# Three-pass fp32r products for 28 more weight units of each mixing layer, with their low parts shared between VectorE and GpSimd

## The reference, cut to what matters

```python
h = rms_norm(x, norm_pre[l]) * (1 + scale) + shift
p = h @ w_in[l]                     # fp32, 1024 rows
(..., r_streams, r_z, g_q, g_k, g_v, g_l, g_z, gate_a, gate_b, gate_c) = split(p)
o_mla = mla_branch(...)             # attention
o_rwkv = rwkv7_branch(...)          # r, k, v, decay and a; a chunked recurrence of 64 tokens
o_gla = gla_branch(...)             # gated linear attention from g_q, g_k, g_v
merged = sigmoid(gate_a)*o_mla + sigmoid(gate_b)*o_rwkv + sigmoid(gate_c)*o_gla
x = x + gate * rms_norm(merged @ w_out[l], norm_post[l])
```

## Time and profile before

| | us |
|---|---|
| median of 3 runs (lowest, highest) | 2012.38 (2011.87, 2013.97) |
| the profiled execution's own time | 2014.74 |
| its span, first to last instruction | 2013.0 |
| TensorE busy | 1929.2 (96%) |
| VectorE busy | 1328.2 (66%) |
| ScalarE busy | 713.8 (35%) |
| GpSimd busy | 97.7 (5%) |
| mean granted TensorE clock | 0.987 of full speed |

### The profile page before, as it was taken

The page is one execution under the profiler, slowest core; times in us unless marked ns, Lnnn a source line. Parts: engine busy times, 40 slices in busy tenths (PEclk is TensorE's granted clock), DMA queues, the critical chain, the costliest instruction groups (busy, mean ns, idle before and its releaser), DMA issues.

```text
span 2013.0 us, 41616 instructions
## 1 busy us (share of the span) xinstructions
PE 1929.2 (96%) x18047; PEld 1783.3 (89%) x18047; DVE 1328.2 (66%) x1722; ACT 713.8 (35%) x1023; POOL 97.7 (5%) x137
## 2 busy tenths in 40 slices
PE   8999999999899999999999999997999998999998
PEld 8988999998599999989887879996998887888997
DVE  7896687747657866864675339676764676428765
ACT  5573433435533331240423123243222234204243
POOL 2000000100400000020000000001002000000000
PEclk9999999999999998999999999998999999999999
DMA  8555478853347794645440236454653540135643
GB/s 216 140 144 157 149 236 266 266 147 116 99 148 258 253 258 106 166 117 154 118 116 6 74 102 173 122 161 104 170 160 102 148 128 22 45 99 147 164 121 111
DMA packets 473063, 291.41 MB, mean 145 GB/s; under 512 B 26679, under 2 KB 467484, under 8 KB 472776
## 3 DMA queue, kind: packets, MB, share of 16 engines
q1 hardware_dynamic: 466688, 262.20, 46.7%
q0 software_dynamic: 5312, 25.32, 3.3%
q10 hardware_dynamic: 904, 1.58, 0.3%
HBM read 288.02 MB, written 1.05 MB: 144 GB/s over the span
## 4 chain that ended last, share of the span: by engine, by line
PE 82%; DVE 13%; ACT 3%; issue 2%; POOL 0%; DMA 0%; DVEq 0%; ACTq 0%; POOLq 0%
PE bank L705 38%; PE bank L1422 6%; PE bank L1424 6%; PE bank L1423 6%; PE bank L694 4%; PE bank L664 2%; DVE rounded L730 2%; PE bank L901 2%; PE bank L893 2%; PE bank L1625 1%; PE bank L1612 1%; PE bank L1068 1%; PE bank L787 1%; PE bank L1474 1%; PE bank L1593 1%
## 5 line engine op out<-in xcount | busy, mean ns | idle before, releaser
L705 PE MATMUL bank<-rounded 128*128 128x256 f32 (+1 forms) x4584 | 564.2, 284 | 12.0 <-DVE rounded L730 9.4
L705 PEld LDWEIGHTS bank<-rounded 128*128 128x128 f32 (+1 forms) x4584 | 550.6, 189 | 21.2 <-DVE rounded L730 14.6
L730 DVE TENSOR_TENSOR rounded<-arena,rounded 128x1024 fp32r<-128x1024 f32 (+1 forms) x251 | 303.4, 1214 | 86.6 <-ACT rounded L719 80.5
L1422 PE MATMUL bank<-parts 128*128 128x256 f32 x1024 | 290.5, 284 | 1.0 <-DVE parts L2226 1.0
L1424 PE MATMUL bank<-parts 128*128 128x256 f32 x1024 | 289.8, 283 | 0.0
L1423 PE MATMUL bank<-parts 128*128 128x256 f32 x1024 | 289.8, 283 | 0.0
L705 PE MATMUL bank<-common,arena 128*128 128x256 f32 x1280 | 285.4, 380 | 0.0
L705 PEld LDWEIGHTS bank<-common,arena 128*128 128x128 f32 x1280 | 240.1, 189 | 39.8 <-issue 4.8
L770 ACT ACTIVATE arena<-bank 128x512 f32<-128x512 f32 x114 | 67.6, 597 | 436.1 <-PE bank L705 423.1
L1422 PEld LDWEIGHTS bank<-parts 128*128 128x128 f32 x1024 | 196.5, 192 | 1.5 <-issue 1.3
L1423 PEld LDWEIGHTS bank<-parts 128*128 128x128 f32 x1024 | 196.6, 192 | 0.1
(11 more groups left out here) (391 smaller groups left out, 2497.9 us busy)
## 6 DMA issues: line engine op xcount, KB each, us to landing
arena<-in_w_in SPq DMA_DIRECT2D x190, 512.0 KB, 3.8
whole<-in_ffn_w_gate_up SPq DMA_DIRECT2D x44, 1024.0 KB, 5.2
arena<-in_ada_w POOLq DMA_DIRECT2D x32, 768.0 KB, 6.3
whole<-in_ffn_w_down SPq DMA_DIRECT2D x16, 1408.0 KB, 7.0
arena<-in_rec_w_in SPq DMA_DIRECT2D x36, 512.0 KB, 3.8
arena<-in_att_w_qkv SPq DMA_DIRECT2D x24, 512.0 KB, 3.7
arena<-in_rec_w_out SPq DMA_DIRECT2D x16, 512.0 KB, 3.7
arena<-in_mla_w_o SPq DMA_DIRECT2D x16, 512.0 KB, 3.8
```

Of the source, the lines that this page charges most:

```text
L705: last = pe.matmul(psum[s][0:c, m % 2 * T:m % 2 * T + T], w[a][:, k, cols], x[b][:, k, :], start=(k, a, b) == (0, 0, 0), stop=k == job.kt ...
L730: dve.tensor_tensor(raw_view(job_of[u], u, UNIT_LOW), raw, high_view(job_of[u], u).bitcast(F32), ALU.subtract)\
L1422: pe.matmul(bank, w_hi, x_hi, start=start and k == 0, stop=False)
```

## The change

Five streams of each mixing layer get parts and three passes: r (8 units), v (8), gb0 (4), gq (4) and gk (4), 28 units in a layer and 56 in all. All their high parts are cast by ScalarE. The low parts of r are made by VectorE; those of the other four, 20 units in a layer, by GpSimd (`low_g`, kind `"shared"`), which has a semaphore of its own. r, v and gb0 use three high buffers of their own (`KEY_HIGHS`), since `SW` lies in the usual ones; `AA` and `CC` move to the places of `KKDD` and `V_`. TensorE takes one more unit of v ahead of the head sums of `RK`. `HX` is made anew ahead of gq, where it was made anew ahead of gv. The casts of ro's units 0 and 1 move from the first half of gk to its second, behind the wait for `gate_in`. The diff, cut to its core:

```diff
+        KEY_HIGHS = [rounded(UNIT, at=aligned() + n * UNIT) for n in range(HIGHS)]
...
         place[0] = lent
-        AA, SW, CC = (buf(DK, T) for _ in range(3))
+        SW = buf(DK, T)
+        assert place[0] <= lent + HIGHS * UNIT
+        AA, CC = KKDD, V_
         place[0] = lent
...
+        def wait_parts_pe(u):
+
+            low = unit_low_g if job_of[u].high == "shared" else unit_low
+            pe.wait_ge(low.sem, low_at[u] + 1)
...
                 done = unit_high if job_of[u].high == "vector" else unit_high_s
                 if done is unit_high:
                     high_parts(dve, dve.tensor_copy, u, unit_high)
-                dve.wait_ge(done.sem, done.due(dve))
+                dve.wait_ge(done.sem, high_at[u] + 1)
...
+
+        def low_g(jobs):
+
+            for u in (u for j in jobs for u in range(j.first, j.first + j.units)):
+                gp.wait_ge(unit_high_s.sem, high_at[u] + 1)
+                raw = raw_view(job_of[u], u, UNIT_RAW)
+                gp.tensor_tensor(raw_view(job_of[u], u, UNIT_LOW), raw, high_view(job_of[u], u).bitcast(F32), ALU.subtract)\
+                  .then_inc(unit_low_g.sem, 1)
...
-            def proj(name, n, high=None, at=0):
-                return Stream(n, 2 * n, HX if high else H, columns(w, IN_AT[name] + at * COLS), high=high)
+            def proj(name, n, high=None, at=0, highs=None):
+                return Stream(n, 2 * n, HX if high else H, columns(w, IN_AT[name] + at * COLS), high=high, highs=highs)
...
-                "k": proj("k", 4, "vector"), "r": proj("r", 4), "v": proj("v", 4),
-                "gb0": proj("gb", 2), "gb1": proj("gb", 1, at=2), "gb2": proj("gb", 1, at=3),
+                "k": proj("k", 4, "vector"), "r": proj("r", 4, "scalar", highs=KEY_HIGHS), "v": proj("v", 4, "shared", highs=KEY_HIGHS),
+                "gb0": proj("gb", 2, "shared", highs=KEY_HIGHS), "gb1": proj("gb", 1, at=2), "gb2": proj("gb", 1, at=3),
                 "rz0": proj("rz", 2), "rz1": proj("rz", 1, at=2), "rz2": proj("rz", 1, at=3),
-                "gq": proj("gq", 2), "gk": proj("gk", 2),
+                "gq": proj("gq", 2, "shared"), "gk": proj("gk", 2, "shared"),
...
-        split_left = [list(split_units)]
+        by_gpsimd = [u for u in split_units if job_of[u].high == "shared"]
+        by_vector = [u for u in split_units if job_of[u].high != "shared"]
+        low_at = {u: i for units in (by_gpsimd, by_vector) for i, u in enumerate(units)}
+        cast_by_vector = [u for u in split_units if job_of[u].high == "vector"]
+        cast_by_scalar = [u for u in split_units if job_of[u].high != "vector"]
+        high_at = {u: i for units in (cast_by_vector, cast_by_scalar) for i, u in enumerate(units)}
+        split_left = [list(by_vector)]
         last_split = [rec_zb.through(), att_v[1].through()]
-        high_by_act = [[u for u in split_units if job_of[u].high == "scalar"]]
+        high_by_act = [list(cast_by_scalar)]
...
             multiply_units(j["r"])
             head_sums_pe(SQR, DK, vbanks)
-            multiply_units(j["v"], range(4))
+            multiply_units(j["v"], range(5))
             head_sums_pe(RK, DK, abanks)
-            multiply_units(j["v"], range(4, 8))
+            multiply_units(j["v"], range(5, 8))
             multiply_units(j["gb0"])
             pe.wait_ge(tile_operands.sem, tile_operands.due(pe))
             chunk_tiles_pe(j)
             head_sums_pe(R, DK, vbanks)
+            pe.wait_ge(layer_split.sem, layer_split.due(pe))
             multiply_units(j["gq"], range(2))
             head_sums_pe(SQT, DK, abanks)
             multiply_units(j["gq"], range(2, 4))
...
         def gla_pe(j):
-            pe.wait_ge(layer_split.sem, layer_split.due(pe))
...
+            dve.wait_ge(layer_high_again.sem, layer_high_again.due(dve))
+            dve.tensor_tensor(HX[1], H, HX[0].bitcast(F32), ALU.subtract)\
+               .then_inc(layer_split.sem, 1)
...
             split_v(j["k"].through())
+            split_v(j["r"].first + 1)
             dve.wait_ge(taken[0].sem, halves(0, j["k"]))
             dve.wait_ge(taken[1].sem, halves(1, j["k"]))
             mix_v(raw[0], KR_, DK, 8, l)
+            split_v(j["r"].first + 2)
...
+            split_v(j["r"].first + 3)
             for k in range(DK):
+                if k == DK // 2:
+                    split_v(j["r"].first + 4)
                 dve.tensor_tensor_scan(CC[:, k, :], const("run"), SW[:, k, :], 0.0, ALU.mult, ALU.add)\
                    .then_inc(vector_step.sem, 1)
                 dve.wait_ge(vector_step.sem, vector_step.due(dve))
             dve.tensor_tensor(SW, CC, SW, ALU.subtract)\
...
+            split_v(j["r"].first + 5)
...
+            split_v(j["r"].first + 6)
+            split_v(j["r"].through())
...
-            merge_v(j["ro"], TMP, 3, layer_low)
+            merge_v(j["ro"], TMP, 3)
...
-            take_units(act, j["k"], keep(raw[0], ACT.Copy, 1))
+            take_units(act, j["k"], keep(raw[0], ACT.Copy, 1), only=range(3))
+            high_act(j["r"].first)
+            take_units(act, j["k"], keep(raw[0], ACT.Copy, 1), only=range(3, 4))
+            high_act(j["r"].first + 2)
...
-            take_units(act, j["r"], keep(raw[1], ACT.Copy, 1))
+            take_units(act, j["r"], keep(raw[1], ACT.Copy, 1), high_before(j["r"], 2))
             logarithms_act()
+            high_act(j["v"].first + 2)
...
+            high_act(j["v"].first + 3)
...
+            take_units(act, j["v"], keep(raw[2], ACT.Copy, 1), only=range(1))
+            high_act(j["v"].first + 4)
...
+            high_act(j["v"].first + 5)
...
+            take_units(act, j["v"], keep(raw[2], ACT.Copy, 1), only=range(1, 2))
+            high_act(j["v"].first + 6)
...
+            take_units(act, j["v"], keep(raw[2], ACT.Copy, 1), high_before(j["v"], 2), only=range(2, 4))
...
+            take_units(act, j["gb0"], keep(GT, ACT.Sigmoid), high_before(j["gb0"], 2))
...
+            act.wait_ge(inner_summed.sem, 2 * l + 2)
+            act.activation(HX[0], H, ACT.Copy)\
+               .then_inc(layer_high_again.sem, 1)
+            high_act(j["gq"].first + 2)
+            take_units(act, j["rz2"], keep(ZR[:, 6:], ACT.Silu))
...
-            act.activation(HX[0], H, ACT.Copy)\
-               .then_inc(layer_high_again.sem, 1)
-            take_units(act, j["gq"], keep(GQ, ACT.Copy))
-            take_units(act, j["gk"], keep(GK, ACT.Copy), high_before(j["gk"], 4), only=range(1))
+            take_units(act, j["gq"], keep(GQ, ACT.Copy), high_before(j["gq"], 2))
+            take_units(act, j["gk"], keep(GK, ACT.Copy), high_before(j["gk"], 2), only=range(1))
...
-            take_units(act, j["gk"], keep(GK, ACT.Copy), high_before(j["gk"], 3), only=range(1, 2))
+            take_units(act, j["gk"], keep(GK, ACT.Copy), high_before(j["gk"], 2), only=range(1, 2))
...
                 attend_g(8, MPR, MSM)
+                low_g([second[l][n] for n in ("v", "gb0", "gq", "gk")])
                 add_squares_g(SQM)
```

More of the change, by code:

```diff
@@ L430, in program @@
         unit_landed = [sem(f"unit_landed_{i}") for i in range(RAWS)]
-        unit_high, unit_high_s, unit_low = sem("unit_high_by_vector"), sem("unit_high_by_scalar"), sem("unit_low")
+        unit_high, unit_high_s = sem("unit_high_by_vector"), sem("unit_high_by_scalar")
+        unit_low, unit_low_g = sem("unit_low_by_vector"), sem("unit_low_by_gpsimd")
         unit_used = sem("unit_used")
@@ L653, in first_units_by_pieces @@
             for i in range(2):
-                pe.wait_ge(unit_low.sem, split_at[job.first + i] + 1)
+                wait_parts_pe(job.first + i)
             if rounds:
@@ L672, in multiply_unit @@
             if job.high:
-                pe.wait_ge(unit_low.sem, split_at[u] + 1)
+                wait_parts_pe(u)
                 w = high_view(job, u), raw_view(job, u, UNIT_LOW)
@@ L2879, in rwkv_v @@
             dve.wait_ge(taken[1].sem, halves(1, j["gb2"]))
-            def layer_low(i):
-                if i == 0:
-                    dve.wait_ge(layer_high_again.sem, layer_high_again.due(dve))
-                    dve.tensor_tensor(HX[1], H, HX[0].bitcast(F32), ALU.subtract)\
-                       .then_inc(layer_split.sem, 1)
-            merge_v(j["ro"], TMP, 3, layer_low)
+            merge_v(j["ro"], TMP, 3)
         def gate_in_v(j, l):
@@ L3388, in rwkv_act @@
             act.wait_ge(head_rms.sem, head_rms.due(act))
-            take_units(act, j["v"], keep(raw[2], ACT.Copy, 1), only=range(2))
+            take_units(act, j["v"], keep(raw[2], ACT.Copy, 1), only=range(1, 2))
+            high_act(j["v"].first + 6)
             for k in range(0, DK, 2):
@@ L3396, in rwkv_act @@
                 act.nop().then_inc(bonus_sums.sem, 1)
-            take_units(act, j["v"], keep(raw[2], ACT.Copy, 1), only=range(2, 4))
+            take_units(act, j["v"], keep(raw[2], ACT.Copy, 1), high_before(j["v"], 2), only=range(2, 4))
             act.wait_ge(taken[0].sem, halves(0, j["mo"]))
```

(6 more changed lines are left out.)

## The result

The changed kernel takes 2061.06 us (median of 4 runs, 2058.1 to 2064.94), the kernel before 2013.18 us on the same chip (4 runs, 2011.87 to 2015.12): a ratio of 1.0238, 95% interval 1.0217 to 1.0259. The forecast was 2060 us. The profiled execution took 2059.39 us, with a span of 2057.6 us.

The account below looks back on a forecast made before the run. TensorE was taken to set the pace; shorter products would save 33 us at most, but GpSimd blocking VectorE gives back more: +23.7 us a layer, +47.4 on 2014.74, so 2062, less 2.4 for the median: 2060 us, range 2022 to 2076.

Parts of the forecast that it names:

- waits for r's low parts: In r, TensorE waits for VectorE's low parts: +2.4 us at unit 5, +1.2 at unit 6.
- `tile_operands`: Ahead of the recurrence: 21 us of low parts in VectorE's way, less 5.6 of idle, make it +16 us.
- recurrence: After gb0: TensorE formerly came 3.5 us after `tile_operands`, so it begins at about +12.5 us, unchanged through rz2.
- GpSimd's price: Subtraction of 128x1024 on GpSimd: 2.4 us alone, range 1.9 to 2.9, short enough to keep up with TensorE.
- The blocking: VectorE and GpSimd with SBUF inputs wait for each other's whole operation: about 2.25 us lost by VectorE per low part.
- The case of a slow fp32r result: GpSimd needs 4 us a low part and also paces TensorE in v and gb0: 2110 us; chance 5%.
- The other estimate, 2.36 us: GpSimd's subtraction, halfway between the profile row and the skill page's 4.5 us for 2048 elements; sum by that 2059 us.
- (a): VectorE and GpSimd do run side by side: -4.7 us a layer, 2003 us, faster; chance 13%.
- (b): Blocking is there but shorter, 1.6 us a low part: +11.6 us a layer, 2036 us; chance 12%.
- r's second wait: At r's unit 6, its low part comes 4.1 us later, TensorE needs 2.88 for unit 5: +1.2 us.
- The waits of TensorE: TensorE idle some 6 us or more ahead of the recurrence and some 14 us ahead of ro, released by VectorE.
- ro behind its casts: ro's casts stand behind the gate's exponentials, so ro starts 7.4 us after `branch_ready`, at +23.5 us.

Follow-up runs that it names:

- 64 columns: Changed kernel, GpSimd subtracting 64 of each unit's 128 columns, TensorE taking high parts in place of low for v, gb0, gq, gk: 2031.5 us.
- the multiplication: Changed kernel, GpSimd multiplying 1024 residual columns by ones instead of making low parts, no unit waiting for it, high parts standing in: 2053.0 us.
- run of one column: Changed kernel, GpSimd subtracting 1 of each unit's 128 columns, TensorE taking high parts in place of low for v, gb0, gq, gk: 2006.88 us.

## Why the prediction was right

Step by step, in microseconds later than before, measured from k's start in the second layer:

| step | predicted | measured |
|---|---|---|
| start of r | +2.1 | +1.7 |
| head sums behind r | +1.2 | +1.1 |
| waits for r's low parts | 2.4 and 1.2 | 2.52 and none |
| `tile_operands` | +16 | +14.8 |
| gb0 done | +6 | +7.4 |
| recurrence | +12.5 | +11.3 |
| `SQT`'s sums | +11.3 | +10.6 |
| `branch_ready` | +21.5 | +20.5 |
| ro | +23.5 | +22.4 |
| gv | +23.7 | +22.4 |

- **GpSimd's price.** 2.4 us alone was assumed; 2.39 and 2.40 us are measured where it needn't wait for VectorE. The case of a slow fp32r result is out. (The other estimate, 2.36 us, came as near; but 1024 elements lie a third of the way from 512 to 2048, not halfway, and its sum was worked out with a third.)
- **The blocking.** 2.25 us a low part was GpSimd's own length less 0.15, taken from five operations that met. In the trace after, L2836, L2856, L2859 and L2575 take 2.0 to 2.1 us more than their 2.29: the length less 0.3 to 0.4. The runs with 64 columns (0.98 us more beside 1.29) and with the multiplication (1.7 beside 2.00) say the same. Ahead of `tile_operands` VectorE lost 19.1 us to low parts (nine whole ones and 0.67 us by the one that the clipping cut short), where the prediction counted 21.5.
- **A slip in the sum.** 1.2 + 21 - 5.6 is 16.6, and the prediction went on with 16. With the half microsecond taken off for overlap, that hides half of the 2.4 us: `tile_operands` came only 1.2 us too late in the forecast. It is luck.
- **Rivals (a) and (b).** (a), no blocking, fell with the result, and the lengthened operations show why. The run of one column, in which there is almost nothing to wait for, landed at 2006.88 us where (a) had 2003: about the time that the change would give if the engines did run side by side. The run of 64 columns took 2031.5 us where the steps had 2027: between the two ends they hold to 5 us. (b), a blocking of 1.6 us, is out by the 2.0 to 2.1 us.
- **r's second wait.** It didn't come. Behind the wait of 2.52 us the granted clock was 0.50 from 1628 to 1631, and the three units took 10.28 us instead of 8.7. At the full clock TensorE would have come to unit 6 about 1 us before its low part was there; at the low clock it came about when it was. The 1.6 us lost are thus near the 1.2 forecast, for another reason than the one given.
- **The waits of TensorE.** 3.88 us ahead of the recurrence instead of the 6 announced, and 7.58 us ahead of ro instead of some 14. The missing part is found earlier: 7.09 us for `RK`, which was named only in passing, and 4.52 us for gq3's low part. gk was therefore done at +14.9, not +12. These were waits moved from a later place to an earlier one; the start of ro hangs on VectorE either way.
- **ro behind its casts.** 7.4 us behind `branch_ready` was forecast, 7.5 is measured (304.1 - 296.6).
- **From gq on.** The steps had (23.5 - 12.5) x 2 = 22 us for two layers. The run with gq and gk plain lies 22.2 us lower, and the trace of the second layer has 22.4 - 11.3 = 11.1 us.
- **The sum.** The medians differ by 47.9 us, the steps had 47.4. This nearness has luck in it: gv is 22.4 us late in the second layer and 25.8 in the first, where 23.7 was forecast for both. In the first layer the recurrence begins 11.3 us late as well, but its first two groups of 64 records begin 6.20 us apart instead of 3.94: 2.3 us by the low clock behind TensorE's wait, which no step had. Another 1.7 us is scatter: the kernel before is that much quicker from the recurrence to ro in its first layer than in its second. The steps were 1.3 us too high in one layer and 2.1 too low in the other. (The two profiled spans differ by only 44.6 us, partly because the changed kernel's reached the first mixing layer's k 2.2 us earlier, ahead of everything that the change touches there.)

## What to carry to other kernels

An idle GpSimd is no free help for VectorE where both work from SBUF: here a subtraction that it took over cost VectorE 2.0 to 2.1 us of blocked time, wherever the two met, against the 1.23 us of making it. Ask first what the helper blocks, then what it saves. And splitting a product into cheaper passes paid here as far as the engine that prepares the parts had idle time at the right place: eight units with their casts out of the sigmoids' way gave 9 us and gb0's four another 7.6, while the version that also split the sixteen of v, gq and gk took 38 us more than that one. (12 of the 38 can be the order of r's casts and low parts, which it had from the changed kernel.)

## What was not expected of the hardware

TensorE's clock. Before, it was granted in full (1.00) from r to gb0 and from 1795 to 1836, through gq and gk; after, it fell behind TensorE's gaps. Busy time by stretch in the changed kernel: the gap ahead of gq3, gq3 itself, and what follows (length, PE, PEld, DVE, ACT, POOL, granted clock):

```profile
1849.00:1853.60 4.60, 0.09 (x1) 0.00 (x0) 4.51 (x2) 3.43 (x4) 3.06 (x2) 0.92 0.47 121
1853.60:1859.00 5.40, 5.39 (x24) 5.19 (x24) 5.25 (x5) 0.00 (x0) 4.72 (x2) 0.50 0.01 3
1859.00:1864.00 5.00, 5.00 (x31) 4.39 (x31) 4.82 (x6) 1.54 (x2) 3.25 (x1) 0.93 0.36 105
```

In gq3 the granted clock is 0.50, that is 1.2 GHz, and its 24 records take 5.49 us where the units behind shorter waits take 3.10 at 2.4 GHz. The same follows the 7.09 us ahead of `RK`'s sums (5.30 us instead of 3.60) and the 3.88 us ahead of the recurrence (its first 64 records 1.99 us instead of 1.16). By the Trainium skill (TensorE: Matmul & The Clock Gate, Part 1) the array's clock is gated when it idles, and activity releases it; the rows agree. So a gap costs TensorE more than its length. Part of it didn't reach the end, since VectorE was the bound behind most of these gaps; where TensorE was, at the start of the recurrence, its first and second group of 64 records begin 5.52 us apart (1695.90 to 1701.42) instead of 3.93 us before (1662.06 to 1665.99), and 6.20 us apart in the first layer. Nor does an equal gap always cost the same: with gq and gk plain, the clock behind a wait of 3.9 us was 0.50 in the first layer and 1.00 in the second.
